# A diagonal state space scan: the rounding of its angles and the scaling of its output matrices move from GpSimd to ScalarE

## What the kernel computes

```python
step = jnp.exp(log_step)[:, None]
mag, ang = jnp.exp(lre * step), lim * step
a_re, a_im = mag * jnp.cos(ang), mag * jnp.sin(ang)
...
_, _, s_re, s_im = lax.associative_scan(
    _complex_linear_combine, (a_re_t, a_im_t, bu_re, bu_im), axis=1)
y = (jnp.einsum('blgp,gcp->blgc', s_re, c_re)
     - jnp.einsum('blgp,gcp->blgc', s_im, c_im)
     + d_skip.reshape(SSM_GROUPS, SSM_GROUP) * uf)
z = jax.nn.gelu(y)
return z * jax.nn.sigmoid(z @ w_glu + b_glu)
```

## Time and profile before

| | before |
|---|---|
| median of three runs | 3395.91 us (3383.43 to 3419.63) |
| the profiled execution | 3378.11 us, its span 3376.3 us |
| granted TensorE clock, mean over the span | 0.905 |
| busy: PE, DVE, ACT, POOL | 3037.3, 1696.1, 1091.6, 151.7 us |
| busy from 2500 to 2666 us (15 of the 16 iterations): PE, DVE, ACT, POOL | 159.05, 164.45, 94.41, 124.58 us of 166 |

### The profile page before, as it was taken

One profiled execution on the slowest core, in us unless ns is written; L12 is line 12 of the kernel. 1 busy time (PEld: TensorE's weight loads), 2 busy tenths in 40 slices (PEclk: granted clock), 3 DMA queues, 4 the chain that ended last, 5 costly groups with the idle time before them and its releaser, 6 DMA issues.

```text
span 3376.3 us, 38569 instructions
## 1 busy us (share of the span) xinstructions
PE 3037.3 (90%) x14482; PEld 2513.7 (74%) x14482; DVE 1696.1 (50%) x2788; ACT 1091.6 (32%) x1689; POOL 151.7 (4%) x135
## 2 busy tenths in 40 slices
PE   2999999879999987889887999977789897999999
PEld 1978878779999976777765888744545576888887
DVE  7456785264645645344424444334279853443434
ACT  3332333331221233222324222344446422232222
POOL 0000000000000000000000000000057300000000
PEclk7996898989999997877878999986779997999999
DMA  5111111122333320000101222210112121322222
GB/s 200 51 38 44 51 57 44 38 75 100 127 101 120 112 68 26 32 19 26 38 32 50 94 99 93 93 56 30 39 47 72 50 96 38 99 91 96 95 93 93
DMA packets 68016, 238.18 MB, mean 71 GB/s; under 512 B 7680, under 2 KB 8192, under 8 KB 67776
## 3 DMA queue, kind: packets, MB, share of 16 engines
q1 hardware_dynamic: 64224, 229.23, 20.2%
q10 hardware_dynamic: 3680, 7.42, 0.7%
HBM read 234.52 MB, written 2.10 MB: 70 GB/s over the span
## 4 chain that ended last, share of the span: by engine, by line
PE 79%; DVE 14%; ACT 4%; issue 3%; DMA 0%; ACTq 0%; POOL 0%; SPq 0%; DVEq 0%
PE DP L404 20%; PE DP L405 20%; PE DP L406 20%; PE XP L739 3%; PE XP L878 2%; DVE PAIRS L2115 2%; PE DP L455 1%; PE XP L517 1%; DVE MPROD L464 1%; DVE TQ L544 1%; DVE PR L2103 1%; DVE HL L533 1%; PE XP L752 1%; PE DP L898 1%; PE XP L968 1%
## 5 line engine op out<-in xcount | busy, mean ns | idle before, releaser
L404 PE MATMUL DP<-HH,WL 128*128 128x512 f32 (+1 forms) x1920 | 735.8, 383 | 117.9 <-DVE WL L397 72.3
L405 PE MATMUL DP<-HH,WH 128*128 128x512 f32 (+1 forms) x1920 | 712.8, 371 | 0.0
L406 PE MATMUL DP<-HL,WH 128*128 128x512 f32 (+1 forms) x1920 | 712.7, 371 | 0.0
L397 DVE TENSOR_TENSOR WL<-RAW,WH 128x1024 fp32r<-128x1024 f32 x327 | 402.1, 1230 | 390.5 <-ACT WH L388 381.0
L404 PEld LDWEIGHTS DP<-HH,WL 128*128 128x128 f32 x1920 | 367.4, 191 | 185.7 <-DVE WL L397 78.7
L388 ACT ACTIVATE WH<-RAW 128x1024 fp32r<-128x1024 f32 x327 | 343.7, 1052 | 467.0 <-PE DP L406 410.1
L404 PE MATMUL DP<-AH,WL 128*128 128x384 f32 (+1 forms) x1296 | 476.3, 367 | 18.5 <-DVE AL L2140 11.1
L406 PE MATMUL DP<-AL,WH 128*128 128x384 f32 (+1 forms) x1296 | 471.4, 364 | 0.0
L405 PE MATMUL DP<-AH,WH 128*128 128x384 f32 (+1 forms) x1296 | 471.3, 364 | 0.0
L405 PEld LDWEIGHTS DP<-HH,WH 128*128 128x128 f32 x1920 | 367.3, 191 | 54.6 <-issue 11.1
L406 PEld LDWEIGHTS DP<-HL,WH 128*128 128x128 f32 x1920 | 366.4, 191 | 46.2
(11 more groups left out here) (316 smaller groups left out, 3855.5 us busy)
## 6 DMA issues: line engine op xcount, KB each, us to landing
RAW<-in_stream SPq DMA_DIRECT2D x423, 512.0 KB, 3.5
MATS<-in_ssm ACTq DMA_DIRECT2D x16, 256.0 KB, 2.6
X<-in_x SPq DMA_DIRECT2D x8, 384.0 KB, 9.9
BW<-in_rel ACTq DMA_DIRECT2D x4, 512.0 KB, 3.6
out<-X SPq DMA_DIRECT2D x8, 256.0 KB, 2.7
COND<-in_cond SPq DMA_DIRECT2D x1, 1024.0 KB, 4.8
CONST<-in_const SPq DMA_DIRECT2D x1, 256.0 KB, 4.9
COS<-in_rope SPq DMA_DIRECT2D x1, 256.0 KB, 11.9
```

What stands on the lines that cost most here:

```text
L397: dve.tensor_tensor(WL[:, w, :], RAW[:, nxt.u % RING, :], WH[:, w, :].bitcast(F32), ALU.subtract).then_inc(raw_done[nxt.u % RING], 1)
L404: pe.matmul(out, al, bh, start=first, stop=False)
L405: pe.matmul(out, ah, bh, start=False, stop=False)
L406: return pe.matmul(out, ah, bl, start=False, stop=last)
```

## The change

The rounding becomes two activations on ScalarE, one that adds 1.5 * 2^23 from a new constant tile `ROUND` and one that takes it off again; they stand at the end of `angles(i)`. `outputs_scaled(i)` is cut in two: ScalarE scales the matrices, between its wait for tile i and the gate's sigmoid, and GpSimd keeps the sum, the difference and the negation. ScalarE now waits for all 28 steps of `ssm_prep` ahead of the first angles.

```diff
             def turns(i):
-                pool.wait_ge(sem("turn_scaled"), i + 1)
-                pool.tensor_scalar(TR[:, 0:LAT], TURN[:, :], MAGIC, MAGIC, ALU.add, ALU.subtract
-                                   ).then_inc(sem("turn_steps"), 1)
-                pool.wait_ge(sem("turn_steps"), i + 1)
+                pool.wait_ge(sem("turn_steps"), 2 * i + 2)
                 pool.tensor_tensor(TURN[:, :], TURN[:, :], TR[:, 0:LAT], ALU.subtract).then_inc(sem("ssm_turns"), 1)
             def outputs_scaled(i):
-                pool.wait_ge(sem(f"ssm_mats{i % 2}"), 16 * (i // 2 + 1))
-                if i:
-                    pool.wait_ge(sem("ssm_out"), i)
-                for c, f in ((0, 11), (1, 5)):
-                    pool.tensor_scalar(TQ[:, 0:2, LAT + c * P:LAT + (c + 1) * P], MATS[:, i % 2, 2:4, :],
-                                       PV(f)[:, i:i + 1], None, ALU.mult).then_inc(sem("c_steps"), 1)
                 pool.wait_ge(sem("c_steps"), 2 * i + 2)
...
                 act.activation(TURN[:, :], IOTA[:, :], ACT.Copy, scale=PV(3)[:, i:i + 1]).then_inc(sem("turn_scaled"), 1)
+                act.wait_ge(sem("turn_scaled"), i + 1)
+                act.activation(TR[:, 0:LAT], TURN[:, :], ACT.Identity, bias=ROUND[:, 0:1]).then_inc(sem("turn_steps"), 1)
+                act.wait_ge(sem("turn_steps"), 2 * i + 1)
+                act.activation(TR[:, 0:LAT], TR[:, 0:LAT], ACT.Identity, bias=ROUND[:, 1:2]).then_inc(sem("turn_steps"), 1)
+
+            def outputs_scaled(i):
+                act.wait_ge(sem(f"ssm_mats{i % 2}"), 16 * (i // 2 + 1))
+                if i:
+                    act.wait_ge(sem("ssm_out"), i)
+                for c, f in ((0, 11), (1, 5)):
+                    act.activation(TQ[:, 0:2, LAT + c * P:LAT + (c + 1) * P], MATS[:, i % 2, 2:4, :], ACT.Copy,
+                                   scale=PV(f)[:, i:i + 1]).then_inc(sem("c_steps"), 1)

             act.wait_ge(sem("ssm_loads"), 16)
+            act.wait_ge(sem("ssm_prep"), SSM_PREP)
...
                 wait_group(act, at)
+                outputs_scaled(i)
                 act.activation(GATES[:, i, :], DP[:, bank(at), :], ACT.Sigmoid, bias=vec("b_gate", i)
                                ).then_inc(bank_free[bank(at)], 1)
```

More of the change, by code:

```diff
@@ L220, in backbone_kernel @@
         QUARTER = sb(ctx, "QUARTER", [P, 1])
+        ROUND = sb(ctx, "ROUND", [P, 2])
         SSMP = sb(ctx, "SSMP", [P, 13, 16])
@@ L638, in _ @@
             pool.memset(QUARTER[:, :], TWO_PI / 4.0).then_inc(sem("eps_set"), 1)
+            pool.memset(ROUND[:, 0:1], 1.5 * 2.0 ** 23)
+            pool.memset(ROUND[:, 1:2], -1.5 * 2.0 ** 23).then_inc(sem("eps_set"), 1)
             norm_wait(pool, "post0", "x", KT)
@@ L1120, in _ @@
                 norm_square(act, "pre0", Xk(T), T, k)
-            act.wait_ge(sem("eps_set"), 2)
+            act.wait_ge(sem("eps_set"), 3)
             norm_rstd(act, "pre0", T)
```

## The result

The changed kernel took 3414.88 us (median of 22 runs, 3390.11 to 3436.35), the kernel before 3384.19 (median of 22 runs, 3367.60 to 3419.63). The medians lie 30.69 us apart. The ratio over all these runs, the one that has an interval, is 1.0074, 95% interval 1.0045 to 1.0102: some 25 us slower, 15 to 34. The forecast was 22 us slower, and 3418 in all, counted from the first three runs of the kernel before, whose median was 3395.91. That 3418 lies only 3 us from 3414.88 is luck: the median of the kernel before came out 12 us lower with more runs, and the medians' difference 9 us larger than 22.

A forecast was written before the change was run, and what follows sets the result against it. Bound: PE, with a floor of 10.65 of 11.30 us per iteration, the other 0.65 VectorE's. 16.8 us for 14 iterations, 3 for the start and 2.3 for the end made 22 over 3395.91: 3418, range 3388 to 3448.

The forecast's parts named there:

- The bound, and the order: State space stage: scaling behind the tile's wait delays sums and output products, so PE idles about 1.5 us per iteration.
- T = 12.5: State space stage's period: PE's loop 12.1 us plus 0.4 for the port, between 12.1 and 12.9; t starts the input products.
- The port: GpSimd's first two sums wait for VectorE's PAIRS products at the shared port, between nothing and 0.8 us, taken as 0.4.
- The cover of ScalarE: ScalarE's two new activations, 0.73 us each, cost nothing while 1.4 to 2.2 us of cover before the next tile's end stands.
- The table load: ScalarE's second table load, ahead of the sigmoid: 1.28 us without the 1.38 of draining; with draining T near 12.9.
- The start, +3: Stage's start: constants, second additions and first scalings make the first output products later; +3 us, between 1 and 4.5.
- The end, +2.3: Stage's end: the last output product starts 9.1 us after its tile instead of 6.86, +2.3 us.
- The sum: Whole change: 14 x (12.5 - 11.3) = 16.8, plus 3, plus 2.3: 22 us slower, ends 14 and 29.
- The rival of the falling clock: PE's idle piece of 1.3 to 2.1 us lowers its clock in the stage, 28 us more: 3446; chance 0.20.
- relief: VectorE, relieved of GpSimd, lets the stage come down to PE's floor, 3390 us in all; chance 0.08.
- cancelling: Scaling, sums and hand-overs in the stage take 2.4 us instead of 3.2, no change on balance: 3398; chance 0.08.
- ScalarE as the bound: With L658 late and additions dearer, ScalarE's loop passes 13.3 us in the stage: 33 us slower, 3429; chance 0.06.

The follow-up runs named there:

- experiment 1: The changed kernel with ScalarE's two scalings ahead of its wait for the gate's tile: stage 201.72 us against 216.82, ratio to the kernel before 1.0022.
- Experiment 2: The kernel before with only the rounding moved to ScalarE, the scaling staying on GpSimd: stage 200.88 us against 200.28.
- experiment 3: The kernel before with only the scaling moved to ScalarE, ahead of its wait for the tile: stage 193.72 us, ratios 1.0011 and 0.9994.
- experiment 7: Two kernels: experiment 1 with L658 on 8 of 512 columns, angles scaled by 1e-6, stage 190.48 us; experiment 3 without GpSimd's negation, stage 202.44 us, ratio 1.0020.
- experiment 6: The changed kernel with GpSimd's negation made twice, stage 230.39 us, or three times, stage 240.55 us; no timed ratio.

## Why the prediction was right, step by step

- **The bound, and the order.** Right. The new loop is PE, ScalarE's scaling, GpSimd's sums, PE, in the chain of waits as forecast, and experiment 1 shows that the place of the scaling makes 15.1 of the stage's 16.5 us.
- **T = 12.5.** Measured 12.20 (2518.23 to 2689.05), inside 12.1 to 12.9. The start of the output products, without conflict, was put at t + 3.2, and with the 0.4 of the port conflict at 3.6; it came at t + 3.15. The mis-sized term is first of all the sums. The forecast took 1.83 from the earlier trace rows, where the third took 0.97, and added 0.4. The means after are 0.885, 0.579 and 0.556, 2.02 in all. The third had been slow beside VectorE's two sums (L2106 ran from 2593.71 to 2595.20); behind PAIRS it isn't. The conflict with PAIRS did come, the first sum most of all, 0.885 against 0.45 without them; but the row that priced the three held another conflict already, which went. The hand-over from GpSimd to PE was 0.05 us in the iteration shown (2588.75 to 2588.80) and not 0.2, and that from ScalarE 0.07 and not 0.1. Against these, the output products kept the next tile 3.14 us and not 3.03. 14 x (12.20 - 11.30) = 12.6 instead of 16.8.
- **The port.** The Trainium skill's rule (SBUF — State Buffer, "SBUF: two separate sides"), that the loser blocks for the whole instruction, agrees with the meetings here: in the iteration of experiment 1 the fourth PAIRS product began at 2617.08, beside L658 (2616.82 to 2618.28), took 1.75 us and ended at 2618.83, 0.55 behind L658's end; with L658 cut short the four took 2.94 us instead of 4.00, and no product took over 0.95.
- **The cover of ScalarE.** Right. The additions took 0.725 us each (forecast 0.73), the scalings 501 ns (0.49), and ScalarE still waited 2.48 us for the tile in the iteration shown. Experiment 2 puts the net effect of the rounding's move at 0.6 us of stage, with the scaling left on GpSimd.

```profile
L1496 ACT ACTIVATE TQ<-MATS,SSMP 128x256 f32<-128x256 f32 x28 | 12.7, 501 | 35.8 <-PE DP L407 35.8
...
L1486 ACT ACTIVATE TR<-TURN,ROUND 128x512 f32<-128x512 f32 x13 | 9.4, 725 | 0.4
...
L666 POOL TENSOR_SCALAR TQ<-TQ 128x128 f32<-128x128 f32 x14 | 7.8, 556 | 0.0
```

- **The table load.** Right: 1.28 us (2586.78) and the sigmoid behind it at 2588.07, no draining between.
- **VectorE's wait for WH.** Forecast some 2 us an iteration, measured 26.3 / 14 = 1.9. GpSimd's busy time per iteration: forecast 3.3, measured 3.15.
- **The start, +3.** Mis-sized: +0.5. The first output products did start 2.15 us later against their tile (2514.83 - 2497.38 = 17.45, and 2496.37 - 2481.07 = 15.30 before), in the forecast's 1 to 3. But in the kernel before they ran at a clock of 0.61 and took 5.09 us to the next tile, and after the change 3.40 at 1.00. What the first lost the second gave back. The forecast didn't look at the clock of the earlier trace rows.

```profile
2496.37:2501.46 5.09, 5.09 (x9) 2.23 (x9) 5.09 (x6) 1.78 (x2) 3.11 (x2) 0.61 0.19 52
```

```profile
2514.83:2518.23 3.40, 3.40 (x9) 1.38 (x9) 3.40 (x4) 0.82 (x2) 1.37 (x1) 1.00 0.23 77
```

- **The end, +2.3.** Measured +3.5. The last output products were 2.07 later against their tile (8.93 instead of 6.86), as forecast, and 1.45 more is a fall of the clock that no term had: with no input products behind the last tile, PE waited 2.90 us.

```profile
2697.98 1.22 PE L1028 MATMUL XP<-PAIRS,TQ 128*128 128x512 f32 x1 [2.90 <-POOL TQ L666]
```

```profile
2697.50:2700.90 3.40, 2.92 (x4) 1.38 (x5) 0.00 (x0) 0.00 (x0) 0.42 (x1) 0.50 0.00 0
```

- **The sum.** Stage: 0.5 + 12.6 + 3.5 = 16.5 against 22, inside 14 to 29. That the timed 25 us lies so near to 22 is partly luck: the stage came out 5 us smaller, and 8 us from elsewhere, open in cause, made up for it.
- **The rival of the falling clock.** It didn't come (1.00 in the windows of the 14 iterations): the idle piece was 1.28 us, the lower end of the 1.3 to 2.1 of the forecast. It was close even so. With one negation more, at 1.88 us, it came after 3 of 10 such pieces. Its price was overestimated, 1.7 us a fall and not 3.5, for the clock was low for some 3.4 us and not all through the products.
- **The other rivals.** As accounts of this change, relief, cancelling and ScalarE as the bound are excluded by the period and the chain. Relief is what experiments 3 and 7 got by order: periods of 10.84 and 10.64.

## What to carry to other kernels

Read where a step is queued before asking how long it takes: 0.9 us on a free engine cost 16.5 us here because it stood behind the wait for a tile on which it didn't depend, and with the same instructions one line earlier the whole change cost 1.4. When an engine is relieved, look at which instructions of its neighbour the remaining ones will then meet; taking away one more can put the rest in a worse place. And size the term at the clock and with the company that the operation will have afterwards, not those of the row it is read from.

## What of the hardware was unexpected

- A small GpSimd sum of 128x128 took 0.45 us alone, 1.01 beside PAIRS and up to 1.40 beside VectorE's scans. Of VectorE's instructions, WL rose from 1.21 to a mean of 2.07 us with the subtraction beside it (experiment 7), while the products that read PSUM (`PR`, L2103 before) took 675 ns each in experiment 3 with a part of the subtraction beside them, and 676 in experiment 7.
- Idle pieces of PE of 1.87 to 1.89 us were followed by a lower clock in 3 of 10 cases, of 1.94 in 3 of 9, of 2.48 in 2 of 5 (experiment 6), and one of 2.90 us was; those of 1.28, and one of 2.11 us in the changed kernel, were not. The length of the piece alone doesn't order these rows.
- Some 30 us of scatter, 712 to 742 us, lie in the first block of kernels that differ only behind it or not at all: a change of 0.5% is better measured by the stage's own length.
